# A transformer layer on one core: a new order for the opening, with spread gains, halved first tiles and zero products

## What is computed

```python
def rms_norm(x, gain):
    xf = x.astype(jnp.float32)
    y = xf * lax.rsqrt(jnp.mean(xf * xf, axis=-1, keepdims=True) + RMS_EPS)
    return (y * gain.astype(jnp.float32)).astype(x.dtype)
...
        h = rms_norm(x, pre_mix_norm[l])
        proj = h @ w_in[l]
        q, k, v_a, u, v_s = jnp.split(
            proj, [ATTN_WIDTH, 2 * ATTN_WIDTH, 3 * ATTN_WIDTH, 3 * ATTN_WIDTH + SGU_WIDTH], axis=-1)
```

## Time and profile before

| | us |
|---|---|
| median of 3 runs | 1798.44 |
| lowest and highest | 1798.21, 1800.26 |
| span of the profiled execution (first to last instruction) | 1795.2 |
| TensorE busy in it | 1767.6 |
| VectorE, ScalarE, GpSimd busy | 1148.7, 848.0, 371.2 |

### The profile page before, as it was taken

One profiled execution on the slowest core, in us unless ns is written; L12 is line 12 of the kernel. 1 busy time (PEld: TensorE's weight loads), 2 busy tenths in 40 slices (PEclk: granted clock), 3 DMA queues, 4 the chain that ended last, 5 costly groups with the idle time before them and its releaser, 6 DMA issues.

```text
span 1795.2 us, 24708 instructions
## 1 busy us (share of the span) xinstructions
PE 1767.6 (98%) x9544; PEld 1443.4 (80%) x9544; DVE 1148.7 (64%) x1804; ACT 848.0 (47%) x1604; POOL 371.2 (21%) x433
## 2 busy tenths in 40 slices
PE   7999999999999999999999999999999999999998
PEld 7767888888888877878878787776888998888887
DVE  6655647348436787877778746677546357574848
ACT  5446534234334564564645644545434445352436
POOL 1503011100000046363463640000120012112112
PEclk9999999999999999999999999999999999999999
DMA  7221383944322444443443444233444248849482
GB/s 248 83 60 62 92 245 88 275 123 130 105 94 73 156 134 140 127 144 112 136 140 122 142 156 156 83 114 122 129 153 141 63 154 183 238 102 262 109 215 71
DMA packets 146053, 246.07 MB, mean 137 GB/s; under 512 B 27712, under 2 KB 59904, under 8 KB 145040
## 3 DMA queue, kind: packets, MB, share of 16 engines
q1 hardware_dynamic: 118976, 166.70, 29.7%
q0 software_dynamic: 26096, 75.30, 16.5%
q10 hardware_dynamic: 864, 2.49, 0.3%
HBM read 229.64 MB, written 14.81 MB: 136 GB/s over the span
## 4 chain that ended last, share of the span: by engine, by line
PE 81%; DVE 11%; ACT 3%; DMA 2%; issue 2%; POOL 1%; SPq 0%; DVEq 0%; ACTq 0%; POOLq 0%
PE m L2217 14%; PE m L2219 14%; PE m L2218 14%; PE m L2228 5%; PE m L2230 5%; PE m L2229 5%; PE s L2382 3%; PE m L2329 3%; PE m L2328 3%; PE m L2327 3%; DVE lo L1456 3%; DMA raw<-in_w_up_dram 2%; PE m L2354 1%; PE m L2356 1%; PE m L2355 1%
## 5 line engine op out<-in xcount | busy, mean ns | idle before, releaser
L2217 PE MATMUL m<-hH,hi 128*128 128x512 f32 (+1 forms) x1392 | 530.1, 381 | 2.7 <-DVE hL L1488 1.6
L2219 PE MATMUL m<-hH,lo 128*128 128x512 f32 (+1 forms) x1392 | 509.8, 366 | 0.0
L2218 PE MATMUL m<-hL,hi 128*128 128x512 f32 (+1 forms) x1392 | 509.2, 366 | 0.0
L1456 DVE TENSOR_TENSOR lo<-raw,hi 128x1024 fp32r<-128x1024 f32 (+1 forms) x253 | 319.1, 1271 | 170.2 <-ACT hi L974 169.8
L974 ACT ACTIVATE hi<-raw 128x1024 fp32r<-128x1024 f32 (+1 forms) x253 | 262.1, 1050 | 206.9 <-DMA raw<-in_w_up_dram 97.9
L2217 PEld LDWEIGHTS m<-hH,hi 128*128 128x128 f32 x1392 | 263.5, 189 | 47.2 <-DVE hL L1488 2.5
L2219 PEld LDWEIGHTS m<-hH,lo 128*128 128x128 f32 x1392 | 263.3, 189 | 43.4
L2218 PEld LDWEIGHTS m<-hL,hi 128*128 128x128 f32 x1392 | 263.8, 190 | 38.9
L2228 PE MATMUL m<-hi,hH 128*128 128x512 f32 (+1 forms) x320 | 133.5, 417 | 2.2 <-DVE lo L1456 2.2
L2230 PE MATMUL m<-hi,hL 128*128 128x512 f32 (+1 forms) x320 | 122.4, 383 | 0.0
L2229 PE MATMUL m<-lo,hH 128*128 128x512 f32 (+1 forms) x320 | 122.4, 382 | 0.0
(11 more groups left out here) (354 smaller groups left out, 3114.2 us busy)
## 6 DMA issues: line engine op xcount, KB each, us to landing
raw<-in_w_in_dram SPq DMA_DIRECT2D x72, 512.0 KB, 3.8
wq<-in_w_down_dram POOLq DMA_DIRECT2D x40, 512.0 KB, 10.0
hn<-scr_cs_dram POOLq DMA_DIRECT2D x32, 512.0 KB, 4.2
raw<-in_w_up_dram SPq DMA_DIRECT2D x32, 512.0 KB, 5.8
wq<-in_w_down_dram SPq DMA_DIRECT2D x24, 512.0 KB, 7.2
raw<-in_w_gate_dram SPq DMA_DIRECT2D x44, 256.0 KB, 3.6
raw<-in_w_up_dram SPq DMA_DIRECT2D x44, 256.0 KB, 4.4
raw<-in_w_in_dram SPq DMA_DIRECT2D x33, 256.0 KB, 3.1
```

The lines of the kernel that those rows point to most:

```text
L1456: e.tensor_tensor(d, r, h.bitcast(F32), ALU.subtract).then_inc(s_lo, 1)
L2217: e.matmul(bank, wh[:, kk, c], h[:, k, q], start=k == 0, stop=False)
L2218: e.matmul(bank, wh[:, kk, c], l[:, k, q], start=False, stop=False)
L2219: x = e.matmul(bank, wl[:, kk, c], h[:, k, q], start=False, stop=k == kt - 1)
```

## The change

1. The gain comes as one row of 4 KB. TensorE spreads it: a column of ones (`ONE`, one partition) times the row gives 128 equal rows in the side banks 2 and 3, and VectorE's scaling of tiles 0 to 3 reads the gain there.
2. Tiles 0 and 1 of x come in halves of 512 columns, the left halves on SyncE's queue, the right ones on ScalarE's.
3. ScalarE squares tile 1 too; the squares on VectorE are gone.
4. Three turned halves stand ahead of block q; half 3 is turned before slot 1. Turned halves 0 to 7 use side banks 0 and 1 in turn, since 2 and 3 hold the gain.
5. TensorE multiplies zeros (`LO[5]`, cleared by VectorE) into a bank that block q overwrites: five products, then four, then six.
6. ScalarE issues tile 2 of x behind the rounding of half 2, and tile 3 behind that of half 3.
7. `s_p1` is also the sign for the right half of tile 1, so waits on it count 16 more.

(Each group below is from one engine's program, in the order SyncE, ScalarE, VectorE, GpSimd, TensorE; the first two are common.)

```diff
-    N_S0.append(-1), N_S1.append(-1), N_HN.append(-1), N_TR.extend([(-1, -1), (-1, -1), (2, 3), (4, 5)][t])
+    N_S0.append(-1), N_S1.append(-1), N_HN.append(-1), N_TR.extend([(-1, -1), (-1, 1), (2, 3), (4, 5)][t])
...
+        def turned(i):
+            return side[i % (2 if i < 8 else 4)]
...
+        ONE = PT[1][0:1, 0:128]
...
-            e.dma_start(X[:, 0, :], A["x"][0, 0:128, :]).then_inc(s_x[0], 16)
+            e.dma_start(X[:, 0, 0:512], A["x"][0, 0:128, 0:512]).then_inc(s_x[0], 16)
+            e.dma_start(X[:, 1, 0:512], A["x"][0, 128:256, 0:512]).then_inc(s_x[1], 16)
...
-            e.dma_start(X[:, 1, :], A["x"][0, 128:256, :]).then_inc(s_x[1], 16)
-            e.dma_start(G[0][:, :], A["pre_mix_norm"][0].partition_broadcast(128)).then_inc(s_gain[0], 16)
+            e.dma_start(G[0][0:1, :], A["pre_mix_norm"]).then_inc(s_gain[0], 16)
+            e.dma_start(X[:, 0, 512:1024], A["x"][0, 0:128, 512:1024]).then_inc(s_xr0, 16)
+            e.dma_start(X[:, 1, 512:1024], A["x"][0, 128:256, 512:1024]).then_inc(s_xr1, 16)
             prepare_root()
             norm_squares(0, 1)
-            for t in range(2, 4):
-                e.dma_start(X[:, t, :], A["x"][0, 128 * t:128 * t + 128, :]).then_inc(s_x[t], 16)
-            root(ST_N[1], (s_sq1, 1), s_nrs, True)
-            split_weights(0)
+            norm_squares(1, 1)
             norm_round(0)
             norm_round(1)
+            split_weights(0)
             norm_round(2)
+            e.dma_start(X[:, 2, :], A["x"][0, 256:384, :]).then_inc(s_x[2], 16)
+            split_weights(1)
             norm_round(3)
-            split_weights(1)
+            e.dma_start(X[:, 3, :], A["x"][0, 384:512, :]).then_inc(s_x[3], 16)
             norm_squares(2, 1)
...
+            e.memset(LO[5][:, 0, :].bitcast(F32), 0.0).then_inc(s_zero, 1)
...
-            o.wait_ge(s_x[1], 16)
-            e.tensor_tensor_reduce(HN[1][:, :], X[:, 1, :], X[:, 1, :], 1.0, 0.0, ALU.mult, ALU.add, st(ST_N[1] + 1)).then_inc(s_sq1, 1)
             norm_scale(0)
-            o.wait_ge(s_sq1, 1)
-            norm_scale(1)
+            norm_scale(1, (0,))
             norm_rest(0)
             norm_rest(1)
             split_weights(0)
             norm_rest(2)
+            norm_scale(1, (1,))
+            split_weights(1)
             norm_rest(3)
-            split_weights(1)
             norm_scale(2)
...
+            e.memset(ONE, 1.0).then_inc(s_zero, 1)
...
+            def zeros(n):
+                for _ in range(n):
+                    e.matmul(main[0][:, :], LO[5][:, 0, 0:128], LO[5][:, 0, :], start=True, stop=True)
...
-            for i in range(4):
-                norm_turn(i)
+            o.wait_ge(s_zero, 2)
+            zeros(5)
+            o.wait_ge(s_gain[0], 16)
+            for h in range(2):
+                e.matmul(side[2 + h][:, :], ONE, G[0][0:1, 512 * h:512 * h + 512], start=True, stop=True).then_inc(s_gbc, 1)
+                read["side", 2 + h] = (s_hn, 8)
+            norm_turn(0)
+            norm_turn(1)
+            zeros(4)
+            norm_turn(2)
+            zeros(6)
```

More of the change, by code:

```diff
@@ L566, in build @@
         s_wq, WQ_FROM = s_x, 16
-        s_sq1 = sem("s_sq1")
+        s_xr0, s_zero = sem("s_xr0"), sem("s_zero")
+        s_xr1, P1_FROM = s_p1, 16
+        s_gbc, GBC_FROM = s_zero, 2
         main = [ctx.enter_context(nc.psum_tensor(f"m{i}", [128, 512], F32)) for i in range(4)]
@@ L1007, in norm_round @@
                 dst = (mH if 12 <= n < 14 else hH)[:, 4 * b:4 * b + 4, 128 * t:128 * t + 128]
-                e.activation(dst, side[i % 4][:, :].rearrange("p (k t) -> p k t", k=4), ACT.Copy).then_inc(s_nhi, 1)
+                e.activation(dst, turned(i)[:, :].rearrange("p (k t) -> p k t", k=4), ACT.Copy).then_inc(s_nhi, 1)
             def evacuate(b, i):
@@ L1456, in split_weights, with norm_scale @@
                 e.tensor_tensor(d, r, h.bitcast(F32), ALU.subtract).then_inc(s_lo, 1)
-            def norm_scale(n):
+            def norm_scale(n, halves=(0, 1)):
                 t = n % 4 if n < 12 else n - 12 if n < 14 else (n - 14) % 4
@@ L1462, in norm_scale @@
                 r = st(ST_N[n] + 2)
-                if n < 18:
+                if n < 18 and 0 in halves:
                     o.wait_ge(s_nrs, n + 1)
                     e.reciprocal(r, r).then_inc(*o.own())
-                else:
+                elif n >= 18:
                     o.wait_ge(s_nrp, n - 17)
-                o.wait_ge(s_gain[i % 2], GAIN_LANDED[i])
+                if n >= 4:
+                    o.wait_ge(s_gain[i % 2], GAIN_LANDED[i])
                 if n >= 2:
@@ L1476, in norm_scale @@
                 o.settle()
-                for h in range(2):
+                for h in halves:
                     k = slice(512 * h, 512 * h + 512)
-                    e.scalar_tensor_tensor(out=HN[n % 2][:, k], in0=src[:, k], scalar=r, in1=G[i % 2][:, k], op0=ALU.mult, op1=ALU.mult).then_inc(s_hn, 1)
+                    if n < 4:
+                        o.wait_ge(s_gbc, GBC_FROM + h + 1)
+                    gain = side[2 + h][:, :] if n < 4 else G[i % 2][:, k]
+                    e.scalar_tensor_tensor(out=HN[n % 2][:, k], in0=src[:, k], scalar=r, in1=gain, op0=ALU.mult, op1=ALU.mult).then_inc(s_hn, 1)
             def norm_rest(i):
@@ L1487, in norm_rest @@
                 c = slice(128 * t, 128 * t + 128)
-                e.tensor_tensor(l[:, k, c], side[i % 4][:, :].rearrange("p (k t) -> p k t", k=4), h[:, k, c].bitcast(F32), ALU.subtract).then_inc(s_nlo, 1)
+                e.tensor_tensor(l[:, k, c], turned(i)[:, :].rearrange("p (k t) -> p k t", k=4), h[:, k, c].bitcast(F32), ALU.subtract).then_inc(s_nlo, 1)
             def output_gain(b, i):
@@ L2029, in mixture @@
                 if g == 12:
-                    o.wait_ge(s_p1, 48)
+                    o.wait_ge(s_p1, P1_FROM + 48)
                     o.wait_ge(s_cst, 16)
@@ L2385, in norm_turn @@
                 n, b = i // 2, i % 2
-                claim("side", i % 4)
+                bank = i % (2 if i < 8 else 4)
+                claim("side", bank)
                 o.wait_ge(s_id, 16)
@@ L2390, in norm_turn @@
                     c = 512 * b + 128 * k
-                    x = transpose(side[i % 4][:, 128 * k:128 * k + 128], HN[n % 2][:, c:c + 128])
+                    x = transpose(turned(i)[:, 128 * k:128 * k + 128], HN[n % 2][:, c:c + 128])
                 x.then_inc(s_ntr, 1)
-                read["side", i % 4] = (s_nlo, i + 1)
+                read["side", bank] = (s_nlo, i + 1)
+            def zeros(n):
+                for _ in range(n):
+                    e.matmul(main[0][:, :], LO[5][:, 0, 0:128], LO[5][:, 0, :], start=True, stop=True)
             def mixture(g):
```

6 lines of the change are left out of this document (4 added, 2 removed).

## The result

| | before | changed |
|---|---|---|
| time, median of the runs | 1798.33 us (1796.62 to 1800.26, 4 runs) | 1807.92 us (1805.01 to 1809.14, 4 runs) |
| ratio | 1 | 1.0057, 95% interval 1.0045 to 1.0069 |
| profiled execution: its time, its span | not given, 1795.2 | 1805.01, 1803.2 |
| first product of block q | 13.73 | 13.63 |
| turn 6 | 22.20 | 28.73 |

The change makes the kernel 0.57% slower, about 10 us by the medians. The profiled execution of the changed kernel is the quickest of its four, so its rows show 8.0 us of span, somewhat less than the median does.

A forecast was written before the change was run, and what follows sets the result against it. TensorE, busy 98% of the span, bounds the kernel, so the opening counts by what it moves TensorE's stream. Tile 3's turn at 15.05 + 5.3 + 5.04 = 25.4 adds 3.2: span 1798.4, median 1801.6 us, range 1797.5 to 1806.0.

The forecast's parts named there:

- The first product at 12.95, at 2.4 GHz: Opening of block q: first product 0.8 us earlier than 13.73; a raised clock would save 1.8 us on 18 products.
- The spread: TensorE spreading the gain row: two 512-column products, 0.86 us each or 1.7 at low clock, done by 6.2 to 7.1, costless.
- The issue of tile 3 at 15.05: ScalarE's queue: the load waits for half 3, turned after 12 products, so it is issued at 15.05 instead of some 7.1.
- The transfer, 5.3: Tile 3's load, meeting SyncE's queue: 5.3 us from issue to landing, bounds 3.8 to 7.4.
- Landing to turn 6, 5.04: Tile 3's chain of squares, scaling and rests, including half 4's rest for the shared bank: 5.04 us.
- Turn 6 at 25.4: Transposes of tile 3's first half, in block q: start at 25.4 against 22.20, 3.2 us later.
- Rival 1: Behind the 3.3 us wait in block q the clock falls, 18 slow products return: +1.8, 1803.4 us; chance 0.15.
- Rival 2: Opening: clock still low at the first product, which comes at 14.15; +5.3, 1803.7 us; chance 0.12.
- Rival 3: Block q: tiles come in time, no waits for tiles 2 and 3; 2.2 us earlier, 1796.2 us; chance 0.10.
- Rival 4: Tile 3 lands fast, in 3.2 to 3.8 us: +1.3, 1799.7 us; chance 0.08.
- The end moves along: Behind block q: later supply and waits shift with it, so the +3.2 us reaches the kernel's end.
- From the span to the median: Whole kernel: the median of the runs stays 3.2 us above the profiled span, turning 1798.4 into 1801.6 us.

The follow-up runs named there:

- the rests first: Changed kernel with halves 4 and 5 rounded before tile 3's squares and their rests made before its scaling: 1804.89 us, ratio 1.0036.
- early tiles: Changed kernel with tiles 2 and 3 of x issued behind the root of tile 0 again: 1800.37 us, ratio 1.0021.
- both edits: Changed kernel with tiles 2 and 3 issued early and halves 4 and 5 rounded and subtracted before tile 3's scaling: 1800.95 us, ratio 1.0017.
- fed in time: Changed kernel, tiles 2 and 3 issued early, their squares, scaling, roundings and rests reordered to when inputs are ready: 1797.8 us, ratio 1.0001.
- late tiles: Kernel before with tiles 2 and 3 issued behind the roundings of halves 2 and 3: 1797.33 us, ratio 1.0002.
- the row and the zeros: Kernel before plus zero products and the gain row spread for tiles 0 and 1, gain broadcast later for tiles 2 and 3: 1796.81 us, ratio 1.0000.

## Why the prediction was wrong

It named the right mechanism, place and releaser, and came out at a third of the size: +3.2 us where the profiled execution has +8.0 of span and the medians +9.6. Two steps failed. The first is the sum for turn 6, 15.05 + 5.3 + 5.04 = 25.4: it measured 15.81 + 6.40 + 6.52 = 28.73, and the largest single error in it is lo3, put at 1.22 us and measured at 2.76. The second is the clock behind the wait, which the forecast put at nothing and kept as a rival: it cost 1.28 us in this profile, and 2.1 to 2.7 in the four others with a wait of over 4 us. By its own steps:

- **The first product at 12.95, at 2.4 GHz.** It came at 13.63, at 2.4 GHz. The clock was right. The term that failed here is the landing of the tiles: I divided bytes by the rate, 1.4 us sooner than 5.56 with 0.44 of it given back. With halves the squares began at 5.59, no sooner than before, and those of tile 1 at 8.04 instead of 6.0. The run with whole tiles shows 4.25 and 5.67, so the row of gain does free the engines as I thought and it is the halves that give it back.
- **The spread.** I took two products of 0.86 to 1.7 us. It is four records, 3.77 us together, 1.9 for each half of 512 columns, at the low clock. It ended at 7.65 instead of 6.2 to 7.1, and held the second scaled half in the run with whole tiles. I had priced it as costless; it isn't once the tiles are there.
- **The issue of tile 3 at 15.05.** 15.81, by the later first product. The chain behind it (12 products, turn 3, half 3) held to 0.1 us.
- **The transfer, 5.3.** 6.4 in the profiled execution, 6.4 to 7.1 in four others that issue it as late, and 8.4 in one; inside the bounds of 3.8 to 7.4 except for the last. My value stood near the middle of the bounds. The traffic beside it (positions in thin packets, the spatial weights, unit 3) may be what puts it at the upper end; no run takes that traffic away.
- **Landing to turn 6, 5.04.** 6.52. Only one term of it failed: lo3 at 1.22, taken from an execution in which GpSimd's product ran at another time. I moved VectorE's instruction (from 19.64 in the kernel before to 25.31 in the end) without asking what now stood beside it. In three profiles (this one, the rests first, the kernel unedited again) lo3 began while GpSimd's product ran. It took 2.76, 2.00 and 2.02, and ended 1.08 to 1.09 us behind the end of the product each time: it stood nearly until the product was over. Begun first, it took 1.22 (early tiles), and with the product held back too. The price was to be had beforehand: in the kernel before, the same kind of instruction at 42.13 took 1.98, begun during a product of GpSimd that ended at 43.03. The Trainium skill, "GPSIMD Engine Reference", section "Specifications", says that GpSimd's access to SBUF is shared with VectorE and contends with instructions of VectorE that have two inputs in SBUF. lo3 is one, and the trace agrees: 1.22 alone, 2.76 begun during the product.
- **Turn 6 at 25.4.** The three sum to it: 0.76 + 1.1 + 1.48 = 3.33, and 25.4 + 3.33 = 28.73. All three erred the same way, and I had kept their ends for the range one at a time. Whether one cause moved them together no run shows.
- **Rival 1, the clock.** I gave it 0.15 beside the forecast. It is no alternative to it but follows from it: TensorE waited 5.9 us, the granted clock was 0.58 in the window behind it, and 1.28 us more were lost; behind the waits of 4.70, 5.10, 5.58 and 6.42 in other profiles it was 2.64, 2.68, 2.38 and 2.11 (the time from turn 6 to the end of block q, less 18.14). With the wait of 2.12 us in the run with the rests first it fell too, two products later; behind waits of 1.15 to 1.76 (early tiles, turn 4 of the changed kernel, both edits) it stayed. The wait of 3.3 us that the forecast itself had was longer than one that did cost the clock. Rival 2 (a low clock at the first product) did not come, but the six zeros themselves ran slow in three other executions (GpSimd's product later, whole tiles, the kernel unedited again) and held the first product to 14.6, 14.1 and 14.9.
- **Rival 3, faster.** Its condition (tile 3 landed by 15.0) is what the runs with early tiles fulfil; fed in full, block q ends 1.57 us sooner, near the 2.2 that I gave it, and little of it is seen in the time. Rival 4 (landing in 3.2 to 3.8 us) did not come: 6.4.
- **The end moves along.** Held: 7.81 us at the end of block q, 8.0 in the span; TensorE's later waits, all of those behind 50 us, are 13.0 in sum against 11.1. From the end of block q to the end of the span it takes 1754.9 us before and 1755.1 now, and 1754.6 to 1757.6 in the other profiles, whatever the version, but for the one at a lower clock (last section). So a gain of 1 or 2 us at block q can't be read from one span.
- **From the span to the median.** I kept 3.2 us between them. In the profiles with a time of their own it is 1.8 (1805.01 and 1803.2); the other 1.4 was how far that one execution lay under the median of the first runs. That slip moved the forecast towards the measured time, which was luck. The changed kernel's profiled execution is its quickest, 2.9 below its median. The end of block q varies with it: 48.15 and 50.13 in two executions of the same kernel, the landing of tile 3 and the clock behind the wait differing.

## What to carry to other kernels

An opening is worth what the *last* of its inputs allows. Before a transfer's issue is put behind work on an in-order queue, follow what that work waits for: here a turn moved behind 12 products took the load of tile 3 with it, by 9 us. A chain priced with durations of the old trace needs a second look at each link: what will run beside it at its new time, and what traffic will its transfer meet; where several links can err the same way, take their ends together. And a wait of some us on TensorE should be priced with the clock behind it (here from 2.12 us on): it is a part of the same case.

## What the runs showed of the hardware that I had not expected

- Transposes alone can be enough for the high clock: with late tiles in the kernel before, 16 transposes (8.54 to 12.08) and nothing else stood ahead of the product at 13.63, and its followers are 0.12 us apart; in the kernel before, 16 transposes from 8.64 to 12.29 left the products at 13.73 0.21 apart. The same work, and the level changed between two executions. What decides between them I can't say from these traces.
- With zero products behind a memset at 1.4 us the first product ran at the high level in all eleven profiles (first products at 13.2 to 14.9); without them in one of three. In five of the eleven the last zeros still ran partly or wholly slow.
- The granted clock of the rows doesn't show the low level of the opening: it reads 1.00 from 13.70 to 17.70 in the kernel before, with products 0.21 apart. Behind a wait it does show it: 0.50 from 28.70 to 30.00 in the changed kernel.
- 1 MB of tokens in four halves on two queues was there later than in two whole tiles (squares at 5.59 and 8.04 against 4.25 and 5.67). In the other profiles with halves they begin at 5.3 to 6.5 and 7.4 to 7.9.
- The clock fell behind a wait of 2.12 us of TensorE and stayed behind those of 1.15 to 1.76. Behind the 2.12 it did not fall at once, but after the turn and two products; behind 5.89 the turn itself was slow already (1.11 us, as against 0.60).
- Of a tensor_tensor of VectorE on two SBUF inputs and one of GpSimd, the one that began second was stretched: VectorE's 1.22 to 2.76, 2.00 and 2.02, ending 1.08 to 1.09 us behind GpSimd's; or GpSimd's 2.35 to 3.12 and 2.71 (early tiles, fed in time), where VectorE's had begun first and kept its 1.22.
- The profiled execution with the row and the zeros had a granted clock of 0.948 over its whole span, where the others have 0.995 and more, and was 2.9 us over its median; its products are 0.12 apart all the same. Nothing in the kernel accounts for it; it isn't used as a time.
